# A chunked scan on one Trainium2 core: GpSimd's split of half a weight strip is moved behind VectorE's weighting of the keys, and the scan's tile loads are issued one strip sooner

## What is computed

```python
def hgrn2_chunkwise(q, fpre, v, lb):
    f = lbh + (1.0 - lbh) * jax.nn.sigmoid(fpre)
    k = 1.0 - f
    logf = jnp.log(f)
...
    def step(S, inp):
        b = jnp.cumsum(lfc, axis=2)
        inter = jnp.einsum('bhtd,bhde->bhte', qc * jnp.exp(b), S)
        decay = jnp.exp(jnp.where(mask, diff, -jnp.inf))
        A = jnp.einsum('bhtsd,bhsd->bhts', qc[:, :, :, None, :] * decay, kc)
        intra = jnp.einsum('bhts,bhse->bhte', A, vc)
        S_new = jnp.exp(b_last[:, :, 0, :])[..., None] * S + jnp.einsum(
            'bhsd,bhse->bhde', kc * jnp.exp(b_last - b), vc)
        return S_new, inter + intra
```

## Time and profile before

| what | value |
|---|---|
| median of 3 runs | 3044.17 us (3030.78 to 3044.49) |
| the profiled execution, its own time | 3047.28 us |
| span of the profiled execution | 3045.4 us |
| TensorE busy | 2839.8 us, 93% |
| VectorE busy | 1720.2 us, 56% |
| GpSimd busy | 945.7 us, 31% |
| the scan in the span | from about 1996 to 2650 us |

### The profile page before, as it was taken

The page is one execution under the profiler, slowest core; times in us unless marked ns, Lnnn a source line. Parts: engine busy times, 40 slices in busy tenths (PEclk is TensorE's granted clock), DMA queues, the critical chain, the costliest instruction groups (busy, mean ns, idle before and its releaser), DMA issues.

```text
span 3045.4 us, 34182 instructions
## 1 busy us (share of the span) xinstructions
PE 2839.8 (93%) x14231; PEld 2391.3 (79%) x14231; DVE 1720.2 (56%) x2160; ACT 675.2 (22%) x1063; POOL 945.7 (31%) x510
## 2 busy tenths in 40 slices
PE   6999899979999999999999989999999999989798
PEld 5787799868777787888888877888888888867677
DVE  4799655654422655444444587241666666476456
ACT  3012222223223310000000033111222222234342
POOL 1422000016622532232233336651222222222354
PEclk9999888889999999999999999999999999989899
DMA  3223223225312421111111135642232233345573
GB/s 134 69 91 108 87 83 97 68 75 193 116 42 97 139 86 54 42 50 48 42 42 56 53 134 171 209 128 87 91 100 94 91 105 112 123 156 197 202 267 132
DMA packets 134270, 325.10 MB, mean 107 GB/s; under 512 B 11724, under 2 KB 49508, under 8 KB 133988
## 3 DMA queue, kind: packets, MB, share of 16 engines
q1 hardware_dynamic: 61632, 165.70, 17.1%
q10 hardware_dynamic: 72484, 157.22, 14.4%
HBM read 245.26 MB, written 77.61 MB: 106 GB/s over the span
## 4 chain that ended last, share of the span: by engine, by line
PE 68%; DVE 17%; issue 7%; ACT 4%; DMA 2%; ACTq 1%; POOL 1%; DVEq 0%; POOLq 0%
PE pp L268 21%; PE pp L286 17%; PE pp L471 7%; PE pp L1931 5%; PE pp L2505 3%; PE pp L1176 2%; DVE hg_E L2561 1%; DVE hg_KQ L2567 1%; PE pp L1406 1%; DVE hg_KQ L2568 1%; DMA ret_m<-m_s 1%; PE pp L1837 1%; DVE ffn_cb L2111 1%; PE pp L1429 1%; DVE hgin_b L2321 1%
## 5 line engine op out<-in xcount | busy, mean ns | idle before, releaser
L3082 POOL CAST w_hi<-w_raw 128x1024 fp32r<-128x1024 f32 x252 | 306.4, 1216 | 2004.7 <-PE pp L286 864.5
L3084 POOL TENSOR_TENSOR w_lo<-w_raw,w_hi 128x1024 fp32r<-128x1024 f32 x252 | 644.5, 2558 | 20.2
L286 PE MATMUL pp<-w_hi,act_hi 128*128 128x512 f32 x1344 | 552.1, 411 | 34.1 <-POOL w_lo L3084 14.3
L286 PE MATMUL pp<-w_hi,act_lo 128*128 128x512 f32 x1344 | 535.1, 398 | 0.0
L286 PE MATMUL pp<-w_lo,act_hi 128*128 128x512 f32 x1344 | 533.7, 397 | 0.0
L286 PEld LDWEIGHTS pp<-w_hi,act_hi 128*128 128x128 f32 x1344 | 259.9, 193 | 94.0 <-POOL w_lo L3084 18.9
L286 PEld LDWEIGHTS pp<-w_hi,act_lo 128*128 128x128 f32 x1344 | 258.1, 192 | 59.9
L286 PEld LDWEIGHTS pp<-w_lo,act_hi 128*128 128x128 f32 x1344 | 259.8, 193 | 52.4
L268 PE MATMUL pp<-act_hi,w_hi 128*128 128x512 f32 (+1 forms) x944 | 290.8, 389 | 0.0
L268 PE MATMUL pp<-act_hi,w_lo 128*128 128x512 f32 (+1 forms) x944 | 290.7, 389 | 0.0
L268 PE MATMUL pp<-act_lo,w_hi 128*128 128x512 f32 (+1 forms) x944 | 290.5, 389 | 0.0
(11 more groups left out here) (393 smaller groups left out, 4162.1 us busy)
## 6 DMA issues: line engine op xcount, KB each, us to landing
w_raw<-in_weights SPq DMA_DIRECT2D x292, 512.0 KB, 3.5
z_s<-hg_st ACTq DMA_DIRECT2D x52, 512.0 KB, 2.8
hg_qkb<-hT_s SPq DMA_DIRECT2D x18, 512.0 KB, 7.5
qkvT_s<-mixin_o ACTq DMA_DIRECT2D x12, 512.0 KB, 2.8
gdn_qkv<-qkvT_s ACTq DMA_DIRECT2D x8, 768.0 KB, 5.1
front_x<-in_x ACTq DMA_DIRECT2D x8, 512.0 KB, 5.7
mix_x<-in_x ACTq DMA_DIRECT2D x8, 512.0 KB, 5.6
x_s<-mix_y ACTq DMA_DIRECT2D x8, 512.0 KB, 3.0
```

Source lines behind the costliest of these rows:

```text
L286: last = pe.matmul(dst, a[:, k, t * P:(t + 1) * P], columns(w, j, k, 0, n), start=(k == 0 and a is high and w is w_hi), stop=(k == NK - 1 ...
L3082: pool.tensor_copy(hi, raw).then_inc(w_split, 1)
L3084: pool.tensor_tensor(lo, raw, hi.bitcast(F32), ALU.subtract).then_inc(w_ready, 1)
```

## The change

There are two edits. SyncE issues the tile loads of the scan four halves (one strip) earlier in its own order. GpSimd, before it splits the first half of strip `100 + scan` for `scan` from 1 to 6, waits until VectorE has done `kd` of round `scan`. Strip `100 + scan` is the one that TensorE takes in round `scan + 1`.

```diff
@@ block.sync
             for r in range(NHALVES):
                 h = r % 2
-                scan = r - RAW_AT[FIRST_STRIP["z"] + N_HI + 3]
+                scan = r - RAW_AT[FIRST_STRIP["z"] + N_HI + 2]
                 if scan >= 0 and scan % 4 == 0 and scan // 4 < NT - 2:
                     hg.load_next(sp, scan // 4)
                 sp.wait_ge(w_ready, r + 1)
@@ block.gpsimd
                 elif j == FIRST_STRIP["z"]:
                     after(pool, ffn.norm.L, "lo1", NT - 1)
                     ffn.norm.settled(pool)
+                scan = j - FIRST_STRIP["z"] - N_HI - 1
+                if 1 <= scan < NT - 1:
+                    after(pool, hg.dves, "kd", scan)
                 for i in range(HALVES[j]):
                     r, q = RAW_AT[j] + i, PART_AT[j] + i
```

## The result

The changed kernel takes 3004.9 us (median of 4 runs, 2996.3 to 3006.7) and the kernel before 3040.1 us beside it (4 runs, 3030.8 to 3044.5). The ratio is 0.988, with a 95% interval of 0.985 to 0.992. The medians are 35.2 us apart.

A forecast was written before the change was run, and what follows sets the result against it. TensorE, busy 93% of the span, was taken as the bound, stalled by late VectorE. Six rounds of 3.90 us wait plus 2.40 us clock, 37.8 us, off 3044.17 gave 3006.4 us; own range 3003 to 3012, overall 2993 to 3023.

The forecast's parts named there:

- one stall with two prices: TensorE at level 2, rounds 1 to 6: a 3.90 us wait, then a slower clock costing 2.40 us, both to go.
- The sum: Rounds 1 to 6: six times 3.90 us of wait plus 2.40 us of clock, 37.8 us gained.
- The price of the clock: TensorE's slow matmuls behind the level 2 wait: 2.40 us a round, between 1.87 and 2.79.
- The forecast's own range: Whole kernel: 3003 to 3012 us, from the bounds of the clock's cost, widened by 3 us.
- What stays: TensorE keeps one wait of 0.4 to 0.6 us in rounds 1 to 6; round 7 keeps its 3.9 us.
- Level 2 was put 1.2 us early: VectorE's last level 2 operation ends at 2300.20; TensorE wants it at 2301.42, so its wait goes.
- The cover: VectorE's 10.63 us pause after `kd` hides the moved pair, 8.34 us at most, ending 2.3 us before VectorE resumes.
- The tile loads at nothing: SyncE's tile loads issued one strip sooner: price taken as nothing, at most 7.8 us a round.
- The rival with the clock: TensorE's clock still falls with the small matmuls; only 23.4 us gained, 3020.8 us; chance 8%.
- The slower rival: The moved pair runs into VectorE's tail (normalisation, state updates), VectorE losing up to 5.9 us; 3063 us; chance 4%.

The follow-up runs named there:

- rounds_1_to_3: The changed kernel with GpSimd's new wait for rounds 1 to 3 alone; 3026.8 us, ratio 0.9945 to the kernel before.
- loads_only: The changed kernel without GpSimd's new wait, so only the tile loads moved one strip sooner; 3043.6 us, ratio 0.9998 to the kernel before.
- the other series: The unaltered changed kernel run again beside the kernel before; 3004.2 us against 3044.6, ratio 0.9870.
- behind_kup2: The changed kernel with GpSimd's moved pair waiting for the weighting of level 2 instead of kd; 3030.7 us, ratio 0.9963 to the kernel before.
- behind_kup4: The changed kernel with GpSimd's moved pair waiting for the weighting of level 4 instead of kd; 3015.3 us, ratio 0.9905 to the kernel before.
- wait_only: The changed kernel with the tile loads back at their old place, so only GpSimd's new wait; 3008.6 us, ratio 0.9888 to the kernel before.
- behind_ss: The changed kernel with GpSimd's moved pair waiting for the first operation of VectorE's tail instead of kd; 3043.7 us, ratio 0.9993 to the kernel before.

## Why the prediction was right

- **The mechanism.** The held operations, the wait at level 2 and the clock behind it were one stall with two prices, and both went when four operations of GpSimd left the start of the round. rounds_1_to_3 shows that it holds round by round, loads_only that the other edit has no part in it.
- **The size.** The sum said 37.8 us for six rounds (23.4 of waits, 14.4 of clock). In the profiles the waits fell from 26.2 to 2.7 us, by 23.5, and the bursts' distances by 38.86. The forecast for the median was 3006.4 us; 3004.9 was measured, 3004.2 in the other series. Part of that closeness is luck: the kernel before stood at 3044.17 us when the forecast was made and at 3040.1 beside the change, so the gains measured are 35.2 and 40.4 us, on either side of 37.8.
- **The price of the clock.** The bounds 1.87 and 2.79 us were taken from the chain, whose pieces of level 3 start up to 0.17 us later than in the timeline. By the timeline the six rounds give 2.78, 2.54, 2.40, 2.40, 1.71 and 2.62 us, 14.45 in all, so the 14.4 of the sum holds. The forecast's own range, 3003 to 3012, doesn't follow to the microsecond either: 3044.17 less 40.1 and less 34.6 gives 3004.1 and 3009.6 before the 3 us are added.
- **What stays.** 0.4 to 0.6 us at level 1, as said. In round 7 the wait stayed too, 3.92 us for 3.89, but the round became 1.0 us shorter: the clock behind the wait cost 1.5 us where it had cost 2.5. What sets this price isn't shown. Level 2 was put 1.2 us early and came 1.1 early.
- **The cover.** The pair was bounded at 8.34 us by a row with VectorE at work. It takes 6.96 us alone and ends 3.6 us before VectorE goes on.
- **The tile loads at nothing.** Right for the change. The weak point, had only the wait been made, was sized too well in an expectation: the margin of 2.9 us was used up, mostly by a landing 17.2 us after `kd` instead of 15.
- **The rival with the clock** is refuted by behind_kup2, where the fall moves to level 3 with the pause, and behind_kup4, where a pause of 1.35 us has none. In the changed kernel the levels with the same matmuls run at 1.00.
- **The slower rival.** Its place does take the gain away, but its price was too high: 3063 us was worked out and 3043.7 measured. Two of its terms failed. The loss in the tail was put at 5.9 us and 3.1 were measured: scaling and state update aren't held. And it had VectorE late at level 0 and again at level 2; in fact the tail's loss and the burst's fell together on level 0, one wait of 5.7 us for both. The prediction put the rule of the Trainium skill (SBUF — State Buffer, "Who interferes with whom") too shortly. The page says that a VectorE instruction with at most one input in SBUF doesn't contend with GpSimd when it is outside the 2-port modes, and that one with two contends with a GpSimd instruction that reads SBUF. The trace agrees for the operations with an operand in PSUM. By the short form the tail would have lost almost nothing, and the largest single loss was that of an operation with one input in SBUF, see below.

## What to carry to other kernels

Find where an off-path engine's burst lies against the engine that feeds the bound one. If it holds that engine's operations, ask how much of the burst is needed there at all, and put the rest in a pause of the engine that is held, with an explicit wait. Size the place by slack, since the same pair cost 5.3, 1.6 or 0 us a round in three places. A pause is no good place if the work starts at its end: begun at the tail, right behind the pause, the pair took the whole gain away. Then look at what is queued behind the new wait: a load on another queue had lost all of its margin by it.

## What the runs showed of the hardware

- The clock of TensorE fell to 0.50 (1.2 of 2.4 GHz) with pauses of 3.1, 3.9 and 5.7 us in the scan and not with pauses of 1.35 and of 0.4 to 1.1 us (the longest of these in wait_only). It is low before TensorE starts again, in the last 1.3 us of round 3's pause in the kernel before:

```profile
2304.00:2305.30 1.30, 0.00 (x0) 0.00 (x0) 1.30 (x4) 0.00 (x0) 0.12 (x1) 0.50 0.07 19
```

- The fall cost 1.7 to 2.8 us each time in rounds 1 to 6 of the kernel before, and 1.5 to 3.0 us in those of behind_kup2, behind pauses that all were 3.04 to 3.08 us long. So the price varies with pauses of one length.
- A `TENSOR_SCALAR` of VectorE on 128 x 8 numbers, with one input in SBUF, took 2.27 us instead of 0.17 beside a GpSimd subtraction (L1016 in behind_ss). It ended at 2266.02, and the subtraction at 2263.57 + 2.41 = 2265.98. Two of its neighbours show the same: L1012 ended at 2263.51 and the cast beside it at 2263.49, L1018 at 2266.99 and its cast at 2266.97. So in these rows what an operation loses goes by the end of GpSimd's, not by its own size. The Trainium skill (SBUF — State Buffer, "Who interferes with whom") names `tensor_scalar` among the operations that can enter a 2-port mode and so contend, which agrees; that this one was in such a mode no run here shows.
- In the second recurrence of the kernel before, a reduction with one input in SBUF ran inside GpSimd's subtraction from 2844.93 to 2847.64 and was not held: 1.21 us, as when alone. The small `TENSOR_SCALAR` behind it was: it ended at 2847.68, with the subtraction. The scan's own reduction never lay beside GpSimd.

```profile
2845.32 1.21 DVE L2798 TENSOR_REDUCE ret_sm<-ret_on 128x8 f32<-128x1024 f32 x1
2846.56 1.12 DVE L1007 TENSOR_SCALAR ret_sm<-ret_sm 128x8 f32<-128x8 f32 x1
```

- GpSimd pays too, but less: a cast takes 1.04 us alone and 1.50 between held operations of VectorE, a subtraction 2.39 and 2.73.
